# A two-block transformer kernel on one core: tokens turned by VectorE and SBUF copies where TensorE transposed them

## The chip, the cores and the metric

The kernel runs on one core of one Trainium2 chip. The metric is the device time of one execution in microseconds. Three runs of the kernel before took 2508.69 to 2509.17 us, with a median of 2508.91 us.

## The reference

All values are float32. One sequence of T = 256 tokens with D = 2048 features goes through two blocks, one layer each.

First block: `h = rmsnorm(x)`; `proj = h @ w_in` (2048 x 9216) gives u, v (gated mixing over chunks of 128 tokens, 8 groups), q, k, v (8 heads of 128, stick-breaking attention) and two gates; `merged = sigmoid(g_a) * (y_a @ w_up_a) + sigmoid(g_b) * (y_b @ w_up_b)`; `x += merged @ w_o`; then `x += (silu(gate) * up) @ w_ffn_out` with a hidden width of 5632; then `x += sigmoid(rmsnorm(x) @ w_ple_gate) * (p @ w_ple)`.

Second block: `z = rmsnorm(x) @ w_in_2` feeds a causal convolution of width 3, a pooling branch with trailing means, and cross attention (4 heads) on 256 memory rows; `x += mix @ w_out`; then `u = causal_dwconv(h @ w_up) + b`, `x += (silu(gate) * val) @ w_down`; a last rmsnorm.

Nearly all arithmetic is in the products with the weights, 470 MB of which are read once.

## The kernel before, in words

**The stream.** All weight products are cut into 878 granules of 512 KB (128 partitions x 1024 values). A chunk of 8 granules (22 for the two down projections, 4 for w_up_a and w_up_b, 1 for w_ple and the pooling) gives 512 output columns for all 256 tokens, with the tokens on the partitions, in two PSUM banks. For each granule SP loads it into one of RAW = 6 buffers `raw` (`fetch`), ScalarE rounds it to float32r (`wh`, line 1327), VectorE computes the rest `wl = raw - wh` (line 1328), both in a ring of RING = 4, and TensorE does 12 matmuls of 512 columns (`multiply`, lines 1291 and 1297: hi x hi, hi x lo, lo x hi). The last of a granule, line 1297, signals that its ring slot is free.

**The order.** The program is written by one loop over steps. At step s it emits, each on its own engine's queue: the cast and the rest of granule s; the load of granule s + RAW, which waits for the rest of granule s; all work that was put at step s by `at(s, fn)`; and last the 12 matmuls of granule s - 3. Each queue runs in the order of emission. The cast of granule s waits for the last matmul of granule s - 4. A chunk whose last granule is `last` is drained by its `after` at step s = last + 4.

**Turning.** The next product needs its operand with the features on the partitions. `turn` does that: eight TensorE transposes (four in `after_ffn1`, where a chunk gives 256 useful columns) of 128x128 into PSUM banks 4 to 7 (line 374), put at s + 2 or later. ScalarE and VectorE then read those banks and write the operand's `hi` and `lo` parts. The uses: `after_u` (2 chunks), `after_qk` (4), `after_ub` (4, `merged`), `unfold` (16: the residual chunks of w_o, w_ffn_out and w_out, and those of `after_ple`; it writes x1g, x2g, x4g, x3g), `after_ffn1` (22), `after_z` (8) and `after_ffn2` (22). With four transposes in each of the 22 these are 536 transposes, as much as 67 full turns.

**Stages in order of time:** w_in (18 chunks, with attention beside the last ones), w_up_a/w_up_b by turns, w_o, w_ffn_in, w_ffn_out, w_ple_gate/w_ple, w_kv, w_in2 (7 chunks, cross attention `xhead` and pooling beside), w_out with two pooling products, w_up2, w_down. Where the last chunk of a stage feeds the next one, the granules of the next one take its features in order, so that the last features turned (k = 12 to 15) are needed from the next stage's 7th granule on. `late_loads` fetches 2 MB of memory rows at the change to w_ple_gate.

Of the kernel before, what the change touches and what calls it, by code (L numbers as in the profile page):

```python
# [7 lines left out]
P = 128  # L8
T = 256
# [4 lines left out]
RAW = 6  # L14
RING = 4
# [20 lines left out]
MIX_ORDER = (12, 14, 0, 6, 2, 8, 10, 4)  # L36
# [77 lines left out]
def two_block_kernel(nc, t, out):  # L114
# [5 lines left out]
    with ExitStack() as ctx:  # L120
# [26 lines left out]
        o_i = reserve(512)  # L147
        assert NCONST * 4 <= 2560 and place[0] <= nc.sbuf_usable_end
# [12 lines left out]
        ident = view("ident", [P, P], o_i)  # L161
        TA = tmp[:, 0:1024]
# [22 lines left out]
        def parts(name, off_hi, off_lo, n):  # L185
# [44 lines left out]
            "s_attn", "s_cst", "s_mats", "s_misc", "s_late", "s_mem", "s_out", "s_ident", "s_x", "s_gf"))  # L230
        sp = Queue(sem("s_sp"))
# [304 lines left out]
        def after_u(n):  # L536
            def after(s, chunk):
# [9 lines left out]
                def b():  # L547
                    g["t"] = rows_tok[n] = turn(rows, g["u"], 4, 4)
                    u_tok[n] = [act.do(lambda e, i=i: e.copy(
                        U[:, 4 * n + 2 * i:4 * n + 2 * i + 2, :].rearrange("p k t -> p (k t)"), ps[:, 4 + i, :]), g["t"])  # L550
                        for i in range(2)]
                    bank_free[4], bank_free[5] = u_tok[n]
                a()
                at(s + 2, b)
# [54 lines left out]
        def after_qk(dst, g_ap, n):  # L609
            def after(s, chunk):  # L610
# [27 lines left out]
                def f():  # L638
                    rows_tok[n] = g["t"] = turn(rows, g["r"], 4, 4)
                    for i in range(2):  # L640
                        qk_tok.append(act.do(lambda e, i=i: e.activation(
                            dst[:, 4 * n + 2 * i:4 * n + 2 * i + 2, :].rearrange("p k t -> p (k t)"), ps[:, 4 + i, :],
                            ACT.Copy, scale=g_ap), g["t"], got_mats["gq"]))
                    bank_free[4], bank_free[5] = qk_tok[-2:]
# [4 lines left out]
                at(s + 5, f)  # L649
# [125 lines left out]
        def after_ub(n):  # L775
            def after(s, chunk):
                bk = 4 + 2 * (n % 2)
# [5 lines left out]

                def a():
                    done = st_tok["free"] = turn(ST, m, bk, 4)
                    for i in range(2):
                        c = 4 * n + 2 * i
                        hi_ = merged.hi[:, c:c + 2, :].rearrange("p k t -> p (k t)")
                        lo_ = merged.lo[:, c:c + 2, :].rearrange("p k t -> p (k t)")
                        hi = act.do(lambda e, i=i, hi_=hi_: e.copy(hi_, ps[:, bk + i, :]), done)  # L790
                        tk = dve.do(lambda e, i=i, hi_=hi_, lo_=lo_: e.tensor_tensor(
                            lo_, ps[:, bk + i, :], hi_.bitcast(F32), ALU.subtract), hi)
                        merged.ready[c] = merged.ready[c + 1] = bank_free[bk + i] = tk
                at(s + 2, a)
# [10 lines left out]
        def after_ffn1(n):  # L805
            def after(s, chunk):
                bk = 4 + n % 2
                g = {}
                hi = act1.hi[:, 2 * n:2 * n + 2, :].rearrange("p k t -> p (k t)")
                lo = act1.lo[:, 2 * n:2 * n + 2, :].rearrange("p k t -> p (k t)")  # L810
# [638 lines left out]
```

How the kernel before makes its waits and increments, by code:

```python
    def wait(self, tokens):  # L52
        for token in tokens:
            if token is None:
                continue
            if isinstance(token, list):
                self.wait(token)
                continue
            sem, value = token
            if self.waited.get(sem.name, 0) < value:
                self.waited[sem.name] = value
                self.ops.append(lambda e, s=sem, v=value: e.wait_ge(s, v))
# [1 line left out]
    def do(self, fn, *tokens):  # L64
        self.wait(tokens)
        self.n += 1
        self.ops.append(lambda e: fn(e).then_inc(self.sem, 1))
        return (self.sem, self.n)
# [17 lines left out]
    def load(self, sem, dst, src, *tokens):  # L86
        self.count[sem.name] = self.count.get(sem.name, 0) + 16
        self.queue.plain(lambda e: e.dma_start(dst, src).then_inc(sem, 16), *tokens)
        return (sem, self.count[sem.name])
```

## Time and profile before

| what | value |
|---|---|
| median of 3 runs | 2508.91 us |
| profiled execution, its own time | 2509.36 us |
| its span | 2507.2 us |
| TensorE busy | 2486.9 us (99%) |
| VectorE busy | 1403.4 us (56%) |
| ScalarE busy | 1244.4 us (50%) |
| SP's DMA queue, share of 16 engines | 62.2% |
| granted TensorE clock | 0.999 |

The span is the time from the first to the last instruction of the profiled execution, and its own time is 2.2 us more. Busy times of different engines lie beside each other. A matmul's recorded duration (389 ns) is longer than the distance to the next one, because they are pipelined; the distance between starts tells the pace.

### The profile page before, as it was taken

The numbers are of one execution on the slowest core, as the hardware profiler recorded it, in microseconds if no ns is written. First come the engines' busy times: TensorE is split into PE (matmuls) and PEld (weight loads), VectorE is DVE, ScalarE is ACT, GpSimd is POOL, SyncE is SP. The second block draws the span as 40 slices with busy tenths as digits, with TensorE's granted clock in tenths as the row PEclk, the third lists the DMA queues.
The fourth block names the chain that finished last, engine by engine and source line by source line (L and its number), as shares of the span: only waits on it lengthen the run. The fifth ranks groups of instructions, "written<-read, shape, count | busy, mean of one in ns | idle before, by whom it ended". The sixth has DMA issues, their size and how long they took to land.

```text
span 2507.2 us, 27926 instructions
## 1 busy us (share of the span) xinstructions
PE 2486.9 (99%) x11322; PEld 2065.1 (82%) x11322; DVE 1403.4 (56%) x1668; ACT 1244.4 (50%) x1531; POOL 0.2 (0%) x4
## 2 busy tenths in 40 slices
PE   9999999999999999999999999999999999999998
PEld 7888888888888888888888788888888888888886
DVE  7564555655555455544445654765566665665544
ACT  7554666445444444444445654444555555554443
POOL 0000000000000000000000000000000000000000
PEclk9999999999999999999999999999999999999999
DMA  8656666666666666666666565566666666666663
GB/s 287 185 180 188 193 187 178 192 185 185 187 191 189 189 190 188 192 186 192 192 189 225 171 186 178 168 190 186 180 191 185 184 184 191 185 184 209 194 193 128
DMA packets 131105, 473.55 MB, mean 189 GB/s; under 512 B 14624, under 2 KB 15008, under 8 KB 130720
## 3 DMA queue, kind: packets, MB, share of 16 engines
q1 hardware_dynamic: 130976, 471.77, 62.2%
q8 instruction: 89, 1.46, 0.2%
q14 instruction: 40, 0.33, 0.0%
HBM read 469.61 MB, written 2.10 MB: 188 GB/s over the span
## 4 chain that ended last, share of the span: by engine, by line
PE 98%; ACT 1%; DVE 1%; DMA 0%; issue 0%; SPq 0%; DVEq 0%; ACTq 0%
PE ps L1291 86%; PE ps L1297 8%; PE ps L374 2%; ACT wh L1327 0%; DMA raw<-in_w_in 0%; DVE wl L1328 0%; PE ps L732 0%; PE ps L703 0%; PE ps L748 0%; PE ps L580 0%; PE ps L958 0%; PE ps L994 0%; DVE X L881 0%; DVE tmp L876 0%; PE ps L705 0%
## 5 line engine op out<-in xcount | busy, mean ns | idle before, releaser
L1328 DVE TENSOR_TENSOR wl<-raw,wh 128x1024 fp32r<-128x1024 f32 x877 | 1074.0, 1225 | 1076.9 <-ACT wh L1327 1076.6
L1327 ACT CAST wh<-raw 128x1024 fp32r<-128x1024 f32 x877 | 922.6, 1052 | 1171.4 <-PE ps L1297 1168.1
L1291 PE MATMUL ps<-wh,x1g_hi 128*128 128x512 f32 x704 | 276.1, 392 | 0.0
L1291 PE MATMUL ps<-wh,x4g_hi 128*128 128x512 f32 x704 | 276.0, 392 | 0.0
L1291 PE MATMUL ps<-wh,act_hi 128*128 128x512 f32 x704 | 274.3, 390 | 0.0
L1291 PE MATMUL ps<-wl,x1g_hi 128*128 128x512 f32 x704 | 274.0, 389 | 0.0
L1291 PE MATMUL ps<-wl,x4g_hi 128*128 128x512 f32 x704 | 273.9, 389 | 0.0
L1291 PE MATMUL ps<-wl,act_hi 128*128 128x512 f32 x704 | 273.9, 389 | 0.0
L1291 PE MATMUL ps<-wh,h_hi 128*128 128x512 f32 x576 | 227.0, 394 | 2.3 <-DVE wl L1322 1.3
L1291 PE MATMUL ps<-wl,h_hi 128*128 128x512 f32 x576 | 224.1, 389 | 0.0
L1291 PE MATMUL ps<-wh,x1g_lo 128*128 128x512 f32 x528 | 205.7, 390 | 0.0
L1291 PE MATMUL ps<-wh,x4g_lo 128*128 128x512 f32 x528 | 205.6, 389 | 0.0
L1291 PE MATMUL ps<-wh,act_lo 128*128 128x512 f32 x528 | 205.4, 389 | 0.0
L1291 PE MATMUL ps<-wh,h_lo 128*128 128x512 f32 x432 | 168.4, 390 | 0.0
L1291 PEld LDWEIGHTS ps<-wh,act_hi 128*128 128x128 f32 x704 | 132.1, 188 | 27.3
L1291 PEld LDWEIGHTS ps<-wl,act_hi 128*128 128x128 f32 x704 | 132.2, 188 | 27.2
L1291 PEld LDWEIGHTS ps<-wl,x1g_hi 128*128 128x128 f32 x704 | 132.2, 188 | 26.9
L1291 PEld LDWEIGHTS ps<-wl,x4g_hi 128*128 128x128 f32 x704 | 132.2, 188 | 26.8
L1291 PEld LDWEIGHTS ps<-wh,x1g_hi 128*128 128x128 f32 x704 | 132.2, 188 | 26.8
L1291 PEld LDWEIGHTS ps<-wh,x4g_hi 128*128 128x128 f32 x704 | 132.2, 188 | 26.7
L1291 PEld LDWEIGHTS ps<-wh,h_hi 128*128 128x128 f32 x576 | 108.2, 188 | 24.4 <-DVE wl L1322 1.5
L1291 PEld LDWEIGHTS ps<-wl,h_hi 128*128 128x128 f32 x576 | 108.3, 188 | 21.7
(271 smaller groups left out, 3147.4 us busy)
## 6 DMA issues: line engine op xcount, KB each, us to landing
raw<-in_w_in SPq DMA_DIRECT2D x200, 512.0 KB, 3.6
raw<-in_w_ffn_in SPq DMA_DIRECT2D x176, 512.0 KB, 3.6
raw<-in_w_up SPq DMA_DIRECT2D x176, 512.0 KB, 4.2
raw<-in_w_ffn_out SPq DMA_DIRECT2D x88, 512.0 KB, 3.6
raw<-in_w_down SPq DMA_DIRECT2D x88, 512.0 KB, 3.6
raw<-in_w_o SPq DMA_DIRECT2D x32, 512.0 KB, 3.6
raw<-in_w_ple_gate SPq DMA_DIRECT2D x32, 512.0 KB, 3.6
raw<-in_w_out SPq DMA_DIRECT2D x32, 512.0 KB, 3.6
```

Source lines behind the costliest of these rows:

```text
L374: done = pe.do(lambda e, c=c, b=b, at_=at_: e.transpose(ps[:, bk + c // 2, at_:at_ + P], src[:, b, c * P:(c + 1) * P], ident[:]), tok, ban ...
L1291: return e.matmul(*a, start=s, stop=p, skip_group_check=True)
L1297: pe_tok[i] = pe.do(lambda e: e.matmul(dst, lhs, rhs, start=start, stop=stop, skip_group_check=True))
L1327: hi = act.do(lambda e, r=r, slot=slot: e.copy(wh[:, r, :], raw[:, slot, :]), in_tok[s], free)
L1328: lo_tok[s] = dve.do(lambda e, r=r, slot=slot: e.tensor_tensor(wl[:, r, :], raw[:, slot, :], wh[:, r, :].bitcast(F32), ALU.subtract), hi)
```

## The change

`turn` no longer uses TensorE. Two VectorE transposes of 128x512 (one for each half of the tokens) turn every 32x32 block of the rows inside its own quarter of the partitions and write a buffer Y of 4 KB per partition. Sixteen DMAs on SP's queue, each of 32 partitions x 1 KB in runs of 512 B (32 KB), carry the blocks between the quarters into a buffer Z. They are emitted in four groups of four (`move`): two groups at the step of the turn and two at the next one (`steps` = 2: `after_u`, `after_ub`, `unfold`, `after_z`, 30 turns), or one group at each of four steps (`steps` = 4: `after_qk`, `after_ffn1`, `after_ffn2`, 37 turns). All wait for the second VectorE transpose. ScalarE and VectorE read Z, in SBUF, where they read PSUM. What was at s + 2 is now at s + 1 (the VectorE transposes) and s + 5 (the reading of Z); in `after_ffn1` and `after_ffn2` it is s + 1 and s + 7, in `after_qk` s + 4 and s + 10. `after_ffn1` collects two chunks in ST and turns once for both, and `after_ffn2` first copies Z to Y. Y and Z take the place of two raw buffers: RAW is 4. `xhead`, pooling and convolution start two or three steps later, and w_out takes its operands in another order. The transposes of attention probabilities in `xhead` (line 984) stay on TensorE.

```diff
+RAW = 4
 RING = 4
...
+MIX_ORDER = (12, 14, 0, 6, 8, 10, 2, 4)
 
...
+        o_y = reserve(4096)
+        o_z = reserve(4096)
...
+        Y = view("Y", [P, 1024], o_y)
+        Z = view("Z", [P, 1024], o_z)
+        YF = Y.rearrange("p (c t) -> p c t", c=4)
+        YQ = Y.rearrange("p (q g c j) -> p q g c j", q=4, g=2, c=4)
+        ZT = Z.rearrange("p (g c j) -> p c g j", g=8, c=4)
+        ZA = Z.rearrange("p (g a e) -> p g a e", g=2, a=4)
...
-        def turn(src, tok, bk, n):
-
-            done = None
-            for c in range(n):
-                for b in range(2):
-                    at_ = (c % 2) * T + b * P
-                    done = pe.do(lambda e, c=c, b=b, at_=at_: e.transpose(
-                        ps[:, bk + c // 2, at_:at_ + P], src[:, b, c * P:(c + 1) * P], ident[:]),
-                        tok, bank_free[bk], bank_free[bk + 1] if n > 2 else None, got_mats["ident"])
-            return done
-
-        def turned(bk, c):
-            return ps[:, bk + c // 2, (c % 2) * T:(c % 2 + 1) * T]
+        turned = {"n": 0, "y": [], "z": []}
+
+        def turn(step, src, steps, *tokens):
+
+
+
+
+            sem_ = s_turn[turned["n"] % 4]
+            turned["n"] += 1
+            for b in range(2):
+                done = dve.do(lambda e, b=b: e.transpose(YQ[:, :, b].rearrange("p q c j -> p c q j"),
+                                                         src[:, b, :].rearrange("p (c q j) -> p c q j", c=4, q=4)),
+                              *tokens, turned["y"])
+            turned["rows"] = done
+            moved = turned["y"] = []
+            free = turned["z"]
+
+            def move(a):
+                for q in range(4):
+                    token = loads.load(sem_, ZA[32 * q:32 * q + 32, :, a, :],
+                                       Y[32 * a:32 * a + 32, 256 * q:256 * q + 256].rearrange("p (g e) -> p g e", g=2),
+                                       done, free)
+                if a == 3:
+                    moved.append(token)
+
+            for a in range(4):
+                if a * steps < 4:
+                    move(a)
+                else:
+                    at(step + a * steps // 4, lambda a=a: move(a))
+            return moved
+
+        def tiles(x):
+
+            return x.rearrange("p c (g j) -> p c g j", g=8)
 
         def unfold(s, n, tok, gname, dest, free, norm):
 
-            bk = 6 if norm is norm4 else 4 + 2 * (n % 2)
             g = {}
 
...
             def a():
                 squares(n, tok, norm)
+                g["t"] = turn(s + 1, X[:, :, 512 * n:512 * n + 512], 2, tok)
 
             def b():
-                g["t"] = turn(X[:, :, 512 * n:512 * n + 512], tok, bk, 4)
                 for i in range(4):
                     c = 4 * n + i
-                    hi = act.do(lambda e, c=c, i=i: e.activation(dest.hi[:, c, :], turned(bk, i), ACT.Copy,
-                                                                 scale=gain(gname, c)), g["t"], free())
-                    if i % 2 == 0:
-                        continue
-                    for j in (i - 1, i):
-                        dest.ready[4 * n + j] = dve.do(lambda e, c=4 * n + j, j=j: e.scalar_tensor_tensor(
-                            dest.lo[:, c, :], turned(bk, j), gain(gname, c), dest.hi[:, c, :].bitcast(F32),
-                            ALU.mult, ALU.subtract), hi)
-                bank_free[bk] = bank_free[bk + 1] = [hi, dest.ready[c]]
+                    hi = act.do(lambda e, c=c, i=i: e.activation(tiles(dest.hi[:, c:c + 1, :]), ZT[:, i:i + 1],
+                                                                 ACT.Copy, scale=gain(gname, c)), g["t"], free())
+                    dest.ready[c] = dve.do(lambda e, c=c, i=i: e.scalar_tensor_tensor(
+                        tiles(dest.lo[:, c:c + 1, :]), ZT[:, i:i + 1], gain(gname, c),
+                        tiles(dest.hi[:, c:c + 1, :]).bitcast(F32), ALU.mult, ALU.subtract), hi)
+                turned["z"] = [hi, dest.ready[c]]
 
             at(s + 1, a)
-            at(s + 2, b)
+            at(s + 5, b)
             if n == 3:
                 at(s + 3, lambda: rows_root(norm))
                 at(s + 4, lambda: rows_invert(norm))
...
+                    g["t"] = turn(s + 1, ST, 2, m)
+                    st_tok["free"] = turned["rows"]
+
+                def b():
+                    hi = act.do(lambda e: e.copy(tiles(merged.hi[:, 4 * n:4 * n + 4, :]), ZT), g["t"])
+                    lo = dve.do(lambda e: e.tensor_tensor(
+                        tiles(merged.lo[:, 4 * n:4 * n + 4, :]), ZT,
+                        tiles(merged.hi[:, 4 * n:4 * n + 4, :]).bitcast(F32), ALU.subtract), hi)
+                    turned["z"] = lo
+                    for c in range(4 * n, 4 * n + 4):
+                        merged.ready[c] = lo
+                at(s + 1, a)
+                at(s + 5, b)
...
                 def a():
-                    g["t"] = st_tok["free"] = turn(ST, g["m"], bk, 2)
+                    g["t"] = turn(s + 1, ST, 4, g["m"])
+                    st_tok["free"] = turned["rows"]
 
                 def b():
-                    g["hi"] = act.do(lambda e: e.copy(hi, ps[:, bk, :]), g["t"])
+                    c = 2 * n - 2
+                    g["hi"] = act.do(lambda e: e.copy(tiles(act1.hi[:, c:c + 4, :]), ZT), g["t"])
 
                 def c():
-                    tk = dve.do(lambda e: e.tensor_tensor(lo, ps[:, bk, :], hi.bitcast(F32), ALU.subtract), g["hi"])
-                    bank_free[bk] = tk
-                    act1.ready[2 * n] = act1.ready[2 * n + 1] = tk
-                d = 2 if n == 0 else 0
-                at(s + d, z)
-                at(s + d + 2, a)
-                at(s + d + 2, b)
-                at(s + d + 3, c)
+                    c = 2 * n - 2
+                    tk = dve.do(lambda e: e.tensor_tensor(tiles(act1.lo[:, c:c + 4, :]), ZT,
+                                                          tiles(act1.hi[:, c:c + 4, :]).bitcast(F32), ALU.subtract),
+                                g["hi"])
+                    turned["z"] = tk
+                    for k in range(c, c + 4):
+                        act1.ready[k] = tk
+                z()
+                if n % 2:
+                    at(s + 1, a)
+                    at(s + 7, b)
+                    at(s + 8, c)
...
-                    done = rows2_tok["free"] = turn(rows2, g["st"], 6, 4)
+                    g["t"] = turn(s + 1, rows2, 2, g["st"])
+                    rows2_tok["free"] = turned["rows"]
...
-        x_at = first_z[0].last + RING + 4
-        pool_at = first_z[2].last + RING + 4
+        x_at = first_z[0].last + RING + 6
+        pool_at = first_z[2].last + RING + 6
...
                 def y():
-                    g["t"] = st_tok["free"] = turn(ST, g["st"], bk, 4)
+                    g["t"] = turn(s + 1, ST, 4, g["st"])
+                    st_tok["free"] = turned["rows"]
                 hi = act2.hi[:, 2 * n:2 * n + 2, :].rearrange("p k t -> p (k t)")
                 lo = act2.lo[:, 2 * n:2 * n + 2, :].rearrange("p k t -> p (k t)")
 
                 def a():
-                    g["c"] = [act.do(lambda e, c=c: e.activation(C[:, c, :], F[:, c, :], ACT.Identity,
+                    g["f"] = act.do(lambda e: e.copy(tiles(YF), ZT), g["t"])
+                    g["c"] = [act.do(lambda e, c=c: e.activation(C[:, c, :], YF[:, c, :], ACT.Identity,
                                                                  scale=gain("fconv", 176 + 4 * n + c),
-                                                                 bias=gain("fbias", 4 * n + c)), g["t"], part_tok["tb"])
+                                                                 bias=gain("fbias", 4 * n + c)), g["f"], part_tok["tb"])
                               for c in range(4)]
...
-                w = 3 if n == 0 else 0
-                at(s + w, z)
-                at(s + w + 2, y)
+                z()
+                at(s + 1, y)
                 for i, fn in enumerate((a, b, c_, d, f, h)):
-                    at(s + w + 2 + i, fn)
+                    at(s + 7 + i, fn)
...
         for i in range(RAW):
             load_x(i)
             fetch(i)
+        for i in range(RAW, 6):
+            load_x(i)
```

## Rows read from the trace of the kernel before

**Rows 1.** The page: busy time of an engine; shares of the last chain by line.
```profile
PE 2486.9 (99%) x11322; PEld 2065.1 (82%) x11322; DVE 1403.4 (56%) x1668; ACT 1244.4 (50%) x1531; POOL 0.2 (0%) x4
...
PE ps L1291 86%; PE ps L1297 8%; PE ps L374 2%; ACT wh L1327 0%; DMA raw<-in_w_in 0%; DVE wl L1328 0%; PE ps L732 0%; PE ps L703 0%; PE ps L748 0%; PE ps L580 0%; PE ps L958 0%; PE ps L994 0%; DVE X L881 0%; DVE tmp L876 0%; PE ps L705 0%
```

**Rows 2.** Timeline of PE in w_up2: start us, duration us, line, tiles, count.
```profile
2009.36 0.39 PE L1297 MATMUL ps<-wh,x4g_lo 128*128 128x512 f32 x1
...
2012.08 0.40 PE L1297 MATMUL ps<-wh,x4g_lo 128*128 128x512 f32 x1
2012.31 1.04 PE L374 MATMUL ps<-ident,tmp 128*128 128x128 f32 x8
...
2015.72 0.39 PE L1297 MATMUL ps<-wh,x4g_lo 128*128 128x512 f32 x1
```

**Rows 3.** Line 374 alone (ns min/median/max), and who PE waited for (us, times, longest).
```profile
L374 PE MATMUL ps<-ident,tmp x296: 270/272/273, 456.0 to 2262.5; 128*128 128x128 f32 x148
...
PE ps L374 <- DVE X L881: 3.8, 2, 3.4
```

**Rows 4.** Stretches: us, then busy us of PE, PEld, DVE, ACT, POOL; clock, DMA share, GB/s.
```profile
1341.00:1449.00 108.00, 102.83 (x470) 84.75 (x469) 71.91 (x103) 67.48 (x101) 0.00 (x0) 1.00 0.62 198
...
1757.00:2258.00 501.00, 501.00 (x2299) 416.50 (x2299) 308.85 (x400) 276.64 (x357) 0.00 (x0) 1.00 0.62 186
```

**Rows 5.** The page's costliest groups: busy us, mean ns of one, idle before it and releaser.
```profile
L1328 DVE TENSOR_TENSOR wl<-raw,wh 128x1024 fp32r<-128x1024 f32 x877 | 1074.0, 1225 | 1076.9 <-ACT wh L1327 1076.6
L1327 ACT CAST wh<-raw 128x1024 fp32r<-128x1024 f32 x877 | 922.6, 1052 | 1171.4 <-PE ps L1297 1168.1
```

**Rows 6.** Timelines of ACT and of DVE where w_o gives way to w_ffn_in.
```profile
609.53 1.05 ACT L1327 CAST wh<-raw 128x1024 fp32r<-128x1024 f32 x1 [1.67 <-PE ps L1297]
612.25 1.06 ACT L1327 CAST wh<-raw 128x1024 fp32r<-128x1024 f32 x1 [1.67 <-PE ps L1297]
...
613.34 1.23 DVE L1328 TENSOR_TENSOR wl<-raw,wh 128x1024 fp32r<-128x1024 f32 x1 [0.30 <-ACT wh L1327]
```

**Rows 7.** Groups of instructions on DVE and on ACT, shapes kept apart.
```profile
L989 DVE COPY tmp<-ps 128x512 f32<-128x512 f32 x4 | 2.7, 684 | 0.0
...
L399 DVE SCALAR_TENSOR_TENSOR x1g_lo<-ps,cst,x1g_hi 128x256 fp32r<-128x256 f32 x16 | 6.6, 476 | 0.0
...
L338 ACT ACTIVATE mg_hi<-MR,cst 128x256 fp32r<-128x256 f32 x16 | 6.8, 498 | 0.0
```

**Rows 8.** Timeline of SP's queue at the start: start us, duration us of an issue.
```profile
2.11 0.43 SPq L88 DMA_DIRECT2D XT<-in_xt  x1
2.59 0.43 SPq L88 DMA_DIRECT2D raw<-in_w_in  x1
...
4.89 0.68 SPq L88 DMA_DIRECT2D raw<-in_w_in  x1
...
11.16 0.33 SPq L88 DMA_DIRECT2D raw<-in_w_in  x1
```

**Rows 9.** The DMA view: queue's share; issues with count, KB each, median us to landing.
```profile
q1 hardware_dynamic: 130976, 471.77, 62.2%
...
raw<-in_w_in SPq DMA_DIRECT2D x200, 512.0 KB, 3.6
...
MR<-in_mem SPq DMA_DIRECT2D x1, 2048.0 KB, 9.9
...
ident<-in_ident SPq DMA_DIRECT2D x1, 64.0 KB, 4.8
cst<-in_cst SPq DMA_DIRECT2D x1, 8.0 KB, 1.9
```

**Rows 10.** Timeline of DVE at the starts of w_o and of w_out.
```profile
523.61 1.22 DVE L1328 TENSOR_TENSOR wl<-raw,wh 128x1024 fp32r<-128x1024 f32 x1
...
1666.75 0.48 DVE L1105 TENSOR_SCALAR mix_hi<-ps,cst 128x256 fp32r<-128x256 f32 x1
...
1669.49 1.22 DVE L1328 TENSOR_TENSOR wl<-raw,wh 128x1024 fp32r<-128x1024 f32 x1
```

More of the change, by code:

```diff
@@ L13 @@
 EPS = 1e-6
-RAW = 6
+RAW = 4
 RING = 4
@@ L230, in two_block_kernel @@
             "s_attn", "s_cst", "s_mats", "s_misc", "s_late", "s_mem", "s_out", "s_ident", "s_x", "s_gf"))
+        s_turn = [sem(f"s_turn{i}") for i in range(4)]
         sp = Queue(sem("s_sp"))
@@ L547, in b, with c @@
                 def b():
[L548 to L552, printed above, removed]
-                a()
-                at(s + 2, b)
+                    g["t"] = turn(s + 1, rows, 2, g["u"])
+                    rows_tok[n] = turned["rows"]
+                def c():
+                    u_tok[n] = turned["z"] = act.do(lambda e: e.copy(tiles(U[:, 4 * n:4 * n + 4, :]), ZT), g["t"])
+                a()
+                at(s + 1, b)
+                at(s + 5, c)
             return after
@@ L638, in f, with h @@
                 def f():
[L639 to L644, printed above, removed]
+                    g["t"] = turn(s + 4, rows, 4, g["r"])
+                    rows_tok[n] = turned["rows"]
+                def h():
+                    turned["z"] = act.do(lambda e: e.activation(tiles(dst[:, 4 * n:4 * n + 4, :]), ZT, ACT.Copy,
+                                                                scale=g_ap), g["t"], got_mats["gq"])
+                    qk_tok.append(turned["z"])
                 a()
@@ L648, in after @@
                 at(s + 3, d)
-                at(s + 5, f)
+                at(s + 4, f)
+                at(s + 10, h)
             return after
@@ L782, in after @@
                 m = dve.do(lambda e: e.tensor_tensor(ST, ST, SG[:, n, :, :], ALU.add), tok, ua_tok[n])
+                g = {}
                 def a():
[L785 to L794, printed above, removed]
+                    g["t"] = turn(s + 1, ST, 2, m)
[10 more added lines that the diff above has]
+                at(s + 5, b)
             return after
@@ L816, in z @@
                     g["m"] = [dve.do(lambda e, b=b: e.scalar_tensor_tensor(
-                        ST[:, b, 0:T], banks(chunk)[b][:, T:2 * T], RT[:, b:b + 1], ST[:, b, 0:T], ALU.mult, ALU.mult),
-                        g["s"][b], chunk.done) for b in range(2)]
+                        ST[:, b, h0:h0 + T], banks(chunk)[b][:, T:2 * T], RT[:, b:b + 1], ST[:, b, h0:h0 + T], ALU.mult,
+                        ALU.mult), g["s"][b], chunk.done) for b in range(2)]
                     chunk.drained = g["s"] + g["m"]
                 def a():
-                    g["t"] = st_tok["free"] = turn(ST, g["m"], bk, 2)
+                    g["t"] = turn(s + 1, ST, 4, g["m"])
+                    st_tok["free"] = turned["rows"]
                 def b():
-                    g["hi"] = act.do(lambda e: e.copy(hi, ps[:, bk, :]), g["t"])
+                    c = 2 * n - 2
+                    g["hi"] = act.do(lambda e: e.copy(tiles(act1.hi[:, c:c + 4, :]), ZT), g["t"])
                 def c():
-                    tk = dve.do(lambda e: e.tensor_tensor(lo, ps[:, bk, :], hi.bitcast(F32), ALU.subtract), g["hi"])
-                    bank_free[bk] = tk
-                    act1.ready[2 * n] = act1.ready[2 * n + 1] = tk
-                d = 2 if n == 0 else 0
-                at(s + d, z)
-                at(s + d + 2, a)
-                at(s + d + 2, b)
-                at(s + d + 3, c)
+                    c = 2 * n - 2
[10 more added lines that the diff above has]
+                    at(s + 8, c)
             return after
@@ L869, in z @@
                         st_tok["free"]) for b in range(2)]
-                at(s + (2 if n == 0 else 0), z)
+                z()
             return after
@@ L1093, in two_block_kernel @@
                 if what == "u":
-                    conv_taps(ch.last + RING + 3 + i, j)
+                    conv_taps(ch.last + RING + 6 + i, j)
                 else:
-                    conv_split(ch.last + RING + 3, j)
-        conv_taps(first_z[2].last + RING + 3, 0)
+                    conv_split(ch.last + RING + 6, j)
+        conv_taps(first_z[2].last + RING + 6, 0)
         def after_pool(q):
@@ L1148, in b @@
                         o = dve.do(lambda e, c=c: e.scalar_tensor_tensor(
-                            C[:, c, 1:], F[:, c, 0:T - 1], gain("fconv", 88 + 4 * n + c), C[:, c, 1:],
+                            C[:, c, 1:], YF[:, c, 0:T - 1], gain("fconv", 88 + 4 * n + c), C[:, c, 1:],
                             ALU.mult, ALU.add), g["c"][c])
@@ L1153, in b @@
                         g["o"][c] = dve.do(lambda e, c=c: e.scalar_tensor_tensor(
-                            C[:, c, 2:], F[:, c, 0:T - 2], gain("fconv", 4 * n + c), C[:, c, 2:],
+                            C[:, c, 2:], YF[:, c, 0:T - 2], gain("fconv", 4 * n + c), C[:, c, 2:],
                             ALU.mult, ALU.add), g["o"][c])
-                    bank_free[bk] = bank_free[bk + 1] = [g["c"], g["o"]]
+                    turned["y"] = [g["c"], g["o"]]
                 def c_():
```

33 lines of the change are left out of this document (15 added, 18 removed).

## The prediction

> **What bounds the kernel now.** First the page. TensorE is busy for 99% of the span and the chain that ended last runs through its matmuls; 2% of that chain is line 374, the transposes. VectorE and ScalarE are near one half [rows 1]. Next the pace in steady state: the last matmuls of two granules start at 2009.36 and 2012.08, so a granule takes 2.72 us, and the 878 of them 2388 us. With a turn between them the same distance is 15.72 - 12.08 = 3.64 us, so eight transposes cost the bound engine 0.92 us [rows 2]. The feeders' largest idle time is waiting for TensorE: ScalarE's casts for 1168 us on line 1297, VectorE's rests for 1077 us on those casts [rows 5]. So TensorE sets the time, and a microsecond taken from it is a microsecond of the span, until something else comes late.
>
> **What goes.** The 536 transposes that the code issues (296 of them from `tmp`, 0.27 us each with its drain, one pipelined behind the other [rows 3]) are 67 turns of eight: 67 x 0.92 = 61.6 us. The turns of the w_ple stage also made TensorE wait 3.8 us for an addition on VectorE [rows 3], in a stage where it stands idle 108.00 - 102.83 = 5.2 us [rows 4]. In the changed kernel that addition is waited for by VectorE itself. Gain: 65.4 us.
>
> **What comes on VectorE and ScalarE.** 134 block transposes of 128x512. No row shows one. A copy of that shape takes 0.684 us; an operation on half the columns 0.476 [rows 7], on twice the columns 1.225 [rows 5]. I take the copy, 1.37 us a turn, 92 us in all, and keep 0.95 to 2.45 us as its ends. In w_up2 VectorE is busy 308.85 of 501 us [rows 4]; 1.37 us in each chunk of 21.8 raises 62% to 68%. There ScalarE gets a copy of 1024 columns per chunk, about a cast's 1.05 us [rows 5], on 55%. Both hide behind TensorE: the rest of a granule is ready early. Call 0 the moment TensorE ends granule s - 3. The cast of granule s + 1 starts then (612.25) and its rest ends at 613.34 + 1.23, which is 2.35 [rows 6]; TensorE wants it three granules later, at 8.2. That leaves 5.8 us. If this cover were gone each microsecond more would show; the worst burst, eight operations of 0.48 us in `after_ffn2` followed by the next turn, is 3.8 + 1.4 and is spread over two steps, so it stays inside. The other edits to these engines (one cast of 1024 for two of 512, SBUF for PSUM as a source: 0.498 us for 256 columns from SBUF [rows 7]) are worth some tenths beside TensorE: nothing, whichever way.
>
> **What comes on SP's queue.** 16 issues a turn. They start 0.48 us apart when nothing is waited for (2.11, 2.59), and last 0.33 to 0.68 us [rows 8]; I take 0.47, 7.5 us a turn. They wait for the second block transpose, and SP's next `fetch` stands behind them. In a two-step turn: the transposes end at 2.35 + 1.37 = 3.7; eight issues, a fetch, eight issues; the last one starts at about 11.3. The fetch of granule s + 7 leaves at 11.8 where its rest of s + 3 was ready at 7.8: 4 us late. It lands 3.6 us later [rows 9], at 15.4, and the cast wants it at 6 x 2.72 = 16.3. So four raw buffers hold, with 0.9 us before ScalarE waits and 5.8 more before TensorE does; six buffers would have had 5.4 more. Four-step turns put four issues and a fetch (2.3 us) in a step of 2.72 and keep up. At the start of the kernel the fifth load must now wait for the first rest; until the fifth cast lie three more casts of 1.05 us [rows 5] and six operations of about 0.50 [rows 7] on ScalarE, 6.2 us, against 3.6 to land: nothing.
>
> DMA engines: a turn moves 512 KB, as much as one granule, so 67 more loads on 878. With 62.2% [rows 9] for those, even double time for short packets adds under 10 points: covered.
>
> **What is late next.** In the middle of a stage nobody needs Z soon. At the joints somebody does, since reading Z has moved from step s + 2 to s + 5, by three granules, and what is read must have landed. No row shows a 32 KB move between partitions. 8 KB landed 1.9 us after its issue, 64 KB behind other loads 4.8 [rows 9]. I take 2.5, near the first. Then Z is complete at 11.3 + 2.5 = 13.8; the last features are due when TensorE begins the stage's seventh granule, at 5 x 2.72 = 13.6.
> - w_o to w_ffn_in, w_out to w_up2: two casts of 0.50 and a rest of 0.48 [rows 7] for k = 12, 13: 15.3, late by 1.7 each.
> - w_ffn_out to w_ple_gate: the same, and the 2 MB of memory rows (9.9 us to landing [rows 9]) are issued just before the moves. Up to 4 us of queue; most is worked off by the last move. 2.5.
> - w_up_b to w_o: VectorE's rest of s + 1 ends later, at 524.83 [rows 10], 1.05 after the other joints; then one cast of 1024 and one rest of 1024, 1.05 + 1.23: 17.1, late by 3.5.
> - first chunk of w_in2 to `xhead`: its first product is put at s + 6, ahead of the same granule at 13.6, and needs two copies of 512 columns, 1.1 together: 14.9, late by 1.3.
> - last chunk of w_in2 to w_out: pooling work holds VectorE for 2.75 us (1666.75 to 1669.49 [rows 10]) ahead of the block transposes. The moves end at 14.1, the fetch of s + 7 behind them lands at about 18.5, cast and rest of it end at 20.8, the convolution's rest of 0.68 at 21.5; TensorE wants that at 7 x 2.72 = 19.0. Late by 2.5.
>
> Sum of the waits: 1.7 + 1.7 + 2.5 + 3.5 + 1.3 + 2.5 = 13.2 us. With 0.33 us an issue, 1.9 to landing and the shortest transposes it is about 1; each microsecond by which the last move lands later costs 6.
>
> **The sum.** 2509.36 - 65.4 + 13.2 = 2457.2 for an execution like the profiled one; the median of the runs is 0.45 lower, so 2457.
>
> **A rule weighed.** The turns are now made where a copy of 512 columns takes 0.684 us, against 0.92 us for 1024 columns on TensorE. The Trainium skill ("VectorE: DVE Perf Modes", sections "The three transpose paths" and "Rules for kernel authors") gives 390 ns for a 128x128 transpose on TensorE and 311 ns for 32x32 blocks of that size on VectorE, and advises TensorE for 128x128 where PSUM will do. By its 311 ns a turn would be an estimated 2.5 us on VectorE, each joint 1.1 us later, the time 2464. It speaks against the change as if both engines were equally short of time; the rows say they are not.
>
> **Rivals.**
> - *Block transposes at half the copy's pace.* 1.37 us each, 1.37 later at six joints: +8, so 2465. For: it is a reordering, not a copy, and its writes go in pieces of 32. Against: every 512-column row of VectorE in this trace is near 0.68. 0.12.
> - *The moves land late.* Issues at 0.68 us when the queue is loaded (that is what they took at 4.89 [rows 8]) or 4.8 us to landing: 2 to 4 us more at six joints, 2470 to 2481. For: sixteen small ones on one queue, with loads of 512 KB between. Against: in steady state SP's issues lie 2.7 us apart and find the queue empty. 0.10.
> - *No joint is late.* 2509 - 65 + 1 = 2445. Needs both low ends. 0.04.
> - *SP's queue becomes the bound: slower than before.* In a two-step turn the fetch of s + 7 leaves at 4.2 + 16 X for an issue of X us, and 3.6 + 1.05 + 1.23 later its rest is ready; TensorE wants it at 9 x 2.72 = 24.5. So from X = 0.9 on TensorE stops in every such turn, by 16 us per us of X, and the gain is eaten at 65.4 / 30 = 2.2 us a turn, X = 1.03. At X = 1.05: 30 x 2.4 = 72, the four-step turns 12 more: 2509 - 65 + 13 + 84 = 2541. For: 1072 issues are new, and only four buffers are left to cover them. Against: no issue in the trace lasted over 0.68. 0.03.
> - *The change doesn't bring what it removes.* If casts and rests, not matmuls, set the 2.72 us, the transposes lay in a gap: 2505 to 2513. Against: the distance grew by 0.92 us with them. 0.03.
>
> **Chances and range.** The forecast keeps 0.68. A measurement of this kernel can tell about 0.2% (5 us) from no change. Faster by more than that: 0.68 + 0.12 + 0.10 + 0.04 = 0.94; within it 0.03; slower 0.03. The range goes from 2446, almost no wait, to 2474, half of the late case; that leaves out the slow half of that case, the last two rivals and a little of the low end.
>
> **What would show it.** Right: no line-374 rows; granules 2.72 us apart without exception in w_up2; six short waits of TensorE at the joints, together 5 to 25 us, put down to VectorE's rests of `merged`, `x1g`, `x2g`, `x4g`, `mix` and to ScalarE's copy into Z1; block transposes near 0.68 us; ScalarE waiting for the moves about 2 us in two-step turns. Wrong: waits of TensorE for `wl` in the middle of stages, ScalarE waiting for `raw` by more than 5 us, issues on SP over 0.9 us, or a granule's pace other than 2.72 us (by more traffic in SBUF, say).

## The result and the profile after

The changed kernel takes 2586.89 us (median of 4 runs, 2586.43 to 2590.0) against 2508.9 us before: ratio 1.031, 95% interval 1.030 to 1.033. It is 78 us slower where 52 us faster was forecast. The profiled execution took 2587.17 us, with a span of 2585.4 us and a mean granted clock of 0.985 (0.999 before).

The page's busy times and the shares of the last chain, which answer to [rows 1]:

```profile
PE 2468.1 (95%) x10786; PEld 2026.6 (78%) x10786; DVE 1473.0 (57%) x1787; ACT 1259.3 (49%) x1526; POOL 0.2 (0%) x4
...
PE 67%; DVE 10%; SPq 7%; DMA 7%; ACT 6%; issue 3%; DVEq 0%; ACTq 0%
PE ps L1332 61%; SPq L88 7%; PE ps L1338 5%; DVE wl L1371 5%; ACT wh L1370 3%; DMA Z<-Y 3%; DMA raw<-in_w_up 2%; ACT tmp L1181 1%; DVE tmp L1190 1%; DVE Y L387 1%; DVE tmp L1195 1%; ACT Y L1180 1%; DMA raw<-in_w_ple_gate 0%; DVE tmp L1204 0%; DMA raw<-in_w_out 0%
```

The transposes are gone (10786 matmuls where 11322 were), and the chain now leaves TensorE for a third of the span: it goes through SP's queue, the moves, the copies and the rests. TensorE stands idle 2585.4 - 2468.1 = 117.3 us; before it was 20.3. Whom TensorE waited for (us in total, times, longest), the answer to the last of [rows 3]:

```profile
PE ps L1332 <- DVE wl L1371: 64.4, 42, 3.3
PE ps L1332 <- DVE merged_lo L821: 8.4, 1, 8.4
PE ps L1332 <- DVE x4g_lo L426: 5.4, 1, 5.4
PE ps L1332 <- DVE x1g_lo L426: 5.3, 1, 5.3
PE ps L1332 <- DVE x2g_lo L426: 5.2, 1, 5.2
PE ps L1332 <- DVE mix_lo L1125: 3.7, 1, 3.7
PE ps L1332 <- DVE mix_lo L1149: 3.6, 1, 3.6
PE ps L999 <- ACT Z L959: 3.4, 1, 3.4
```

The last seven are at the joints, where one stage gives way to the next: 35.0 us. The first is in the middle of stages, and 48.0 of its 64.4 us lie in w_up2. One stage and a piece of it, as in [rows 4] (us; busy us of PE, PEld, DVE, ACT, POOL; clock; DMA share; GB/s):

```profile
1775.00:2330.00 555.00, 501.63 (x2123) 402.84 (x2122) 328.58 (x438) 292.52 (x374) 0.00 (x0) 0.98 0.61 188
...
1901.00:1926.00 25.00, 22.09 (x85) 17.63 (x84) 13.80 (x20) 12.93 (x17) 0.00 (x0) 0.86 0.59 173
...
1912.00:1916.00 4.00, 4.00 (x11) 3.04 (x11) 4.00 (x7) 2.52 (x3) 0.00 (x0) 0.50 0.39 122
```

w_up2 takes 555 us where it took 501, and there are stretches in which TensorE was granted the lower of its two levels, 1.2 GHz (0.50 in the last row). A mean of 0.985 over 2585 us is 39 us of work lost to half clock. Where TensorE neither waits nor is slowed, a granule takes 2.72 us as before. The distance between the first two of these rows shows it, and the third is one of the waits:

```profile
2005.73 0.39 PE L1338 MATMUL ps<-wh,x4g_lo 128*128 128x512 f32 x1
...
2008.45 0.39 PE L1338 MATMUL ps<-wh,x4g_lo 128*128 128x512 f32 x1
2010.52 0.50 PE L1332 MATMUL ps<-wh,x4g_hi 128*128 128x512 f32 x1 [1.68 <-DVE wl L1371]
```

What the new operations cost: first the block transposes (busy, mean ns), then SP's issues of moves and of loads (ns min/median/max), the answers to [rows 7] and [rows 8], and the DMA view's row of the moves:

```profile
L387 DVE STREAM_TRANSPOSE Y<-tmp 128x512 f32<-128x512 f32 x74 | 48.0, 686 | 0.0
```

```profile
L88 SPq DMA_DIRECT2D Z<-Y x1072: 585/596/2017, 82.8 to 2355.5; - x179
...
L88 SPq DMA_DIRECT2D raw<-in_w_up x176: 327/432/1669, 1760.2 to 2313.4; - x176
```

```profile
Z<-Y SPq DMA_DIRECT2D x1072, 32.0 KB, 2.4
```

The transposes cost 0.686 us (forecast 0.684), a move lands 2.4 us after its issue (forecast 2.5), and an issue holds SP for 0.60 us and the 0.04 after it (forecast 0.47).

### The profile page after: what moved, and what is told of

It reads as the page before. It is cut to its first block, busy times and chain, and to the rows that moved or that the text cites. A ratio compares the mean times of both kernels' runs of the same rounds, so it can differ in the third digit from the quotient of the medians.

```text
span 2585.4 us, 28127 instructions
## 1 busy us (share of the span) xinstructions
PE 2468.1 (95%) x10786; PEld 2026.6 (78%) x10786; DVE 1473.0 (57%) x1787; ACT 1259.3 (49%) x1526; POOL 0.2 (0%) x4
## 4 chain that ended last, share of the span: by engine, by line
PE 67%; DVE 10%; SPq 7%; DMA 7%; ACT 6%; issue 3%; DVEq 0%; ACTq 0%
PE ps L1332 61%; SPq L88 7%; PE ps L1338 5%; DVE wl L1371 5%; ACT wh L1370 3%; DMA Z<-Y 3%; DMA raw<-in_w_up 2%; ACT tmp L1181 1%; DVE tmp L1190 1%; DVE Y L387 1%; DVE tmp L1195 1%; ACT Y L1180 1%; DMA raw<-in_w_ple_gate 0%; DVE tmp L1204 0%; DMA raw<-in_w_out 0%
## 5 line engine op out<-in xcount | busy, mean ns | idle before, releaser
L1370 ACT CAST wh<-raw 128x1024 fp32r<-128x1024 f32 x877 | 912.2, 1047 | 952.8 <-PE ps L1338 799.8
L1332 PE MATMUL ps<-wh,x4g_hi 128*128 128x512 f32 x704 | 282.4, 401 | 53.4 <-DVE wl L1371 48.0
L1332 PEld LDWEIGHTS ps<-wl,h_hi 128*128 128x128 f32 x576 | 108.2, 188 | 21.8
```

Of the source, the lines that this page charges most:

```text
L1332: return e.matmul(*a, start=s, stop=p, skip_group_check=True)
L1370: hi = act.do(lambda e, r=r, slot=slot: e.copy(wh[:, r, :], raw[:, slot, :]), in_tok[s], free)
```

## The experiments

All times are medians, beside runs of the kernel before on the same chip. The last column tells how long w_up2 takes. Its 176 granules at 2.72 us are 478.7 us, so 478.9 means that nothing is lost there.

| kernel | us | against before | first to last start of `wh,x4g_hi` (w_up2), us |
|---|---|---|---|
| before | 2508.9 | | 498.1 |
| changed | 2586.9 | +78.0 | 552.2 |
| before_raw4 | 2509.0 | +0.1 | 498.1 |
| four_moves | 2453.2 | -55.7 | 478.9 |
| joints_pe | 2542.4 | +33.6 | 540.8 |
| up2_pe | 2532.7 | +23.9 | 504.9 |
| joints_up2_pe | 2491.7 | -17.3 | 498.5 |
| split_queues | 2465.2 | -43.8 | 483.2 |
| pool_joints | 2537.4 | +28.5 | 543.8 |
| turn_first | 2528.6 | +19.7 | 500.9 |
| diagonal_pool | 2498.0 | -10.9 | 510.8 |
| split_joints | 2456.5 | -52.5 | 485.6 |
| split_two_joints | 2461.0 | -47.9 | 483.4 |
| split_joints_first | 2448.6 | -60.3 | 478.9 |

**Four raw buffers alone (before_raw4).**

```diff
-RAW = 6
+RAW = 4
...
         for i in range(RAW):
             load_x(i)
             fetch(i)
+        for i in range(RAW, 6):
+            load_x(i)
```

> The kernel before with four raw buffers in place of six, nothing else. Theory A (the sixteen issues of a turn on SP, 0.63 us each, are what makes loads and moves late): four buffers alone cost nothing, 2507 to 2512 us. Theory B (the ring of four raw buffers is too short by itself): TensorE waits for wl in the middle of stages here too, 2520 us or more.

2509.0 us, ratio 1.000 (0.999 to 1.001). The ring of four costs nothing where SP only loads. Theory B falls.

**A quarter of the issues, the same bytes (four_moves).**

```diff
             def move(a):
-                for q in range(4):
-                    token = loads.load(sem_, ZA[32 * q:32 * q + 32, :, a, :],
-                                       Y[32 * a:32 * a + 32, 256 * q:256 * q + 256].rearrange("p (g e) -> p g e", g=2),
-                                       done, free)
+                token = loads.load(sem_, ZA[:, :, a, :],
+                                   Y[:, 256 * a:256 * a + 256].rearrange("p (g e) -> p g e", g=2), done, free)
```

> The changed kernel, with the sixteen moves of a turn replaced by four DMAs over all 128 partitions: the same bytes, the same runs of 512 B, a quarter of the issues. It leaves out that the blocks cross between the partition quarters. Theory A (issues): 12 x 0.63 = 7.6 us less of SP's queue in each turn, the waits for wl in w_up2 (48 us) vanish, the waits at the joints fall from 35 us to under 5, no half clock is left: 2445 to 2460 us. Theory B' (bytes and short packets on the DMA engines, or the time to landing): 2560 to 2590 us, waits as they are.

2453.2 us, ratio 0.978 (0.976 to 0.980), mean clock 0.997. Its issues on SP and its largest waits of TensorE:

```profile
L88 SPq DMA_DIRECT2D Z<-Y x268: 594/600/1649, 82.8 to 2215.7; - x134
...
L88 SPq DMA_DIRECT2D raw<-in_w_up x176: 327/328/433, 1705.4 to 2183.5; - x176
```

```profile
PE ps L1330 <- DVE x2g_lo L424: 4.7, 1, 4.7
...
PE ps L1330 <- DVE merged_lo L819: 1.0, 1, 1.0
```

A move of four times the bytes holds SP as long as a small one, 0.60 us. With 12 issues fewer a turn, no wait for `wl` of over 0.4 us is left, and the time is that of the forecast. The bytes, the runs of 512 B, the block transposes and the later reading of Z are all still there. So the cause is the number of issues, not the bytes. (The edit leaves out that blocks cross between the quarters, so it shows a time and is no version to use.) One joint stays, w_ffn_out to w_ple_gate with 4.7 us. There the last move was issued 3.8 us after the 2 MB of memory rows and took 9.7 us to land, where the median is 3.9; that the rows hold it up is read from this order and was not tested.

**The joints by TensorE (joints_pe), w_up2 by TensorE (up2_pe).** In the first `unfold` and `after_ub` for n = 3 and `after_z` for the first and last chunk of w_in2 are the code of before; in the second `after_ffn2` is:

```diff
...
+            if n == 3 and norm is not norm4:
+                at(s + 1, a_pe)
+                at(s + 2, b_pe)
+            else:
+                at(s + 1, a)
+                at(s + 5, b)
...
```

> The changed kernel with the six turns at the joints (last chunk of w_up_b, w_o, w_ffn_out and w_out, first and last chunk of w_in2) done by TensorE as before. Theory A with the clock as an effect of waits: the 35 us of waits at the joints go, 6 x 0.92 = 5.5 us of transposes come, and the stretches of half clock that begin behind these waits go too, some 15 to 20 us: 2535 to 2545 us. If the half clock has another cause than the waits: 2555 to 2560 us. w_up2 stays at about 550 us.

> The changed kernel with the 22 turns of w_up2 done by TensorE as before, all else as changed. Theory A (in w_up2 a loop of moves, copy, rests and loads takes longer than a chunk's 21.8 us): w_up2 goes from 552 to about 505 us (22 x 0.92 = 20 us of transposes, the joint's wait and its half clock stay): 2535 to 2545 us. If w_up2 is slow by the ring of four buffers and not by the turns: its waits for wl stay, 2570 us or more.

2542.4 us (ratio 1.013, 1.011 to 1.015), as expected: 44.5 us less. By their pages TensorE stands idle 85.0 us where it was 117.3. It is busy 2455.6 us where it was 2468.1, although it does 5.5 us of transposes more: those 18 us are clock, whose mean went from 0.985 to 0.994. Apart from the six turns only waits were taken away, so the half clock was mostly an effect of the waits. That the transposes on TensorE aren't what lifts the clock is seen in four_moves, which has none of these and 0.997. up2_pe gave 2532.7 us (1.009, 1.007 to 1.011), 54 us less and 2 us under what was expected. Both together, joints_up2_pe:

> The six joints and the 22 turns of w_up2 on TensorE, the other 39 turns by VectorE and moves on SP. The two edits gained 44.5 and 54.2 us apart; they touch different stretches, so together 2587 - 44.5 - 54.2 = 2488 us, 21 us under the kernel before. If the waits of the one only moved to the other: 2500 us or more.

2491.7 us (0.993, 0.992 to 0.995): the two gains add up within 4 us. This hybrid beats the kernel before without any new queue.

**Half of the moves from GpSimd (split_queues), all of them (pool_joints, with the joints on TensorE).**

```diff
...
+                    on, sm = (pool_loads, semg) if q % 2 else (loads, sem_)
-                    token = loads.load(sem_, ZA[32 * q:32 * q + 32, :, a, :],
+                    token = on.load(sm, ZA[32 * q:32 * q + 32, :, a, :],
...
```

> The changed kernel with half of a turn's sixteen moves issued by GpSimd's queue, which is otherwise empty; same bytes, same sixteen DMAs, same order and waits. Theory A (time that SP's queue is held by issues): SP then has 8 x 0.63 = 5.1 us less per turn, a step of two moves and a fetch takes 1.9 us, and the waits for wl in w_up2 go. If GpSimd issues a move in 1 us or less: 2450 to 2470 us. If it takes 1.5 us or more, the last move is late by that queue instead: 2480 to 2540 us. Rival (sixteen DMAs are dear in themselves, wherever they are issued, by their completions or packets): 2570 us or more.

2465.2 us (0.982, 0.981 to 0.984). The same sixteen DMAs, shared by two queues, give 122 of the 130 us back by which the forecast had missed. It isn't the DMAs; it is the line in which they stand. A move took longer to land than in the changed kernel (3.7 us on either queue, median, where it was 2.4), and the time fell all the same.

> All sixteen moves on GpSimd's queue, the six joints on TensorE. SP then only fetches. Theory A in its narrow form (SP's loads behind the moves do the harm): 2450 to 2460 us even with slow issues, since only Z is late, and within a stage nobody needs it soon. If late moves hold ScalarE's queue (its copy of Z stands before the next casts), it grows with GpSimd's issue time: at 1 us each the moves end 3.7 + 16 + 2.5 = 22 us after the turn where Z is read at 12 to 17.4, and the time is 2500 to 2600 us.

2537.4 us (1.011, 1.010 to 1.013), the second case, though not by its arithmetic: that asked for 1 us an issue, and GpSimd took 0.53. SP's loads were never behind a move here, and it is just 5 us better than joints_pe. So a late Z is enough for the harm. One turn of w_up2 in its chain of waits (start us, us, what), and the issues:

```profile
1989.89 1.30 DVE Y L390 x2
...
1993.45 7.87 POOL Z L88 x15
2001.33 5.34 DMA Z<-Y
...
2006.69 1.06 ACT Y L1259
```

```profile
L88 POOL DMA_DIRECT2D Z<-Y x16: 533/536/541, 1993.5 to 2001.3; - x16
```

GpSimd issues faster than SP (0.53 us), but in this turn it began 2.3 us after the transposes and its last move took 5.3 us to land beside SP's loads. From the start of the transposes to a complete Z it is 16.8 us. This is one of the four late starts among the 22 turns of w_up2; in the other 18 GpSimd began 0.3 us after the transposes. Even so the copy of Z began about 14 us after their end (median), as in joints_pe: what the quicker issues gave, the slower landing took.

**The loop.** Since both ways of being late ended in the same place, the chain of the changed kernel was followed through one chunk of w_up2:

```profile
2003.04 2.04 DMA Z<-Y
...
2005.10 1.06 ACT Y L1180
...
2006.69 1.58 ACT tmp L1181 x3
2008.27 0.95 ACT wh L1370
...
2009.24 1.22 DVE wl L1371
2010.46 1.58 DVE tmp L1190 x4
2012.04 1.24 DVE tmp L1195 x4
...
2014.67 1.30 DVE Y L387 x2
...
2018.55 4.16 DMA raw<-in_w_up
...
2022.73 1.06 ACT wh L1370
...
2023.81 1.24 DVE wl L1371
2025.05 0.43 SPq L88
...
2025.82 0.58 SPq L88
...
2027.72 2.24 DMA Z<-Y
```

And SP's queue beside it (start us, us, count):

```profile
2016.00 2.51 SPq L88 DMA_DIRECT2D Z<-Y  x4
2018.55 0.58 SPq L88 DMA_DIRECT2D raw<-in_w_up  x1
2019.18 2.50 SPq L88 DMA_DIRECT2D Z<-Y  x4
```

Z is complete at 2005.08; then come the copy to Y, the activations, a cast, its rest, the eight taps, another rest, and only at 2014.67 the block transposes of the next chunk, since they stand behind the taps on VectorE and write the Y that the taps read. Then four groups of moves with a load between, 3.17 us a group; the last group also waits for a rest whose raw load left late at 2018.55. The next Z is complete at about 2030. From Z to Z that is 25 us, and over the whole of w_up2 the block transposes follow each other every 25.2 us (median). TensorE needs 21.8. A wait of ScalarE in front of the copy (22 times, 65.8 us, the DMA's) therefore isn't absorbed: each chunk starts where the last one ended.

Two stages of the same kernel side by side show that it is the loop and not the pace of the groups alone. These are the shares of the chain of work that ended last, first in w_up2 (1850 to 2320 us; its smallest shares are not printed), then in w_ffn_in (640 to 1090 us):

```profile
by line: DVE wl L1371 17.9%; SPq L88 13.6%; DMA raw<-in_w_up 12.1%; DMA Z<-Y 10.2%; issue 8.0%; ACT wh L1370 7.4%; ACT tmp L1181 6.5%; DVE tmp L1190 6.4%; DVE tmp L1195 5.0%; DVE Y L387 4.4%; ACT Y L1180 4.3%; DVE tmp L1204 2.0%; PE ps L133
...
by line: PE ps L1332 91.7%; PE ps L1338 8.3%
```

In w_up2 TensorE's matmuls are about 2% of the chain: it closes without them. In w_ffn_in the turns are four-step turns too, with the same 3.2 us a group (they start at 667.35, 670.54, 673.71 and 676.88), and TensorE never waits for `wl` there. A turn comes only every 16 granules, 43.5 us, and no chunk needs the Z of the turn before for its own transposes.

**The loop cut, with all issues left on SP (turn_first).**

```diff
+        YA = view("YA", [P, 4, T], o_b + 84 * K)
...
-                    g["f"] = act.do(lambda e: e.copy(tiles(YF), ZT), g["t"])
+                    g["f"] = act.do(lambda e: e.copy(tiles(YG), ZT), g["t"], ya_tok.get("free"))
...
-                    g["t"] = turn(s + 1, ST, 4, g["st"])
+                    g["t"] = turn(s + (n > 20), ST, 4, g["st"])
...
-                at(s + 1, y)
+                if n > 20:
+                    at(s + 1, y)
+                else:
+                    y()
```

> The changed kernel with one edit in w_up2 alone: the copy of Z goes to 4 KB of their own (the end of act2's lo part, unused until the last chunks) and not back into Y, and the block transposes of a chunk are put at step s, ahead of the eight taps of the chunk before, not behind them. All sixteen moves stay on SP with their 0.63 us, the ring stays at four. Theory C (a closed loop: transposes, 16 issues, landing, copy, activations, rest, taps, and only then the next transposes, longer than the 21.8 us of a chunk): the loop is cut, a late Z no longer makes the next one later, and w_up2 falls from 555 to 485 to 500 us, the whole to 2520 to 2535. Theory A in its open form (SP's issues hold back the loads through the ring of four, loop or no loop): w_up2 stays over 530 us, the whole over 2560.

2528.6 us (1.008, 1.006 to 1.009); w_up2's first to last start falls from 552.2 to 500.9 us. TensorE's waits for `wl` in the whole kernel, against 64.4 before the edit:

```profile
PE ps L1342 <- DVE wl L1381: 24.4, 25, 3.3
```

58 us come back without one issue less. The copy of Z waits for moves in 2 of the 22 turns where it waited in all, and the block transposes are 22.5 us apart (median), not 25.2. Theory C is shown for w_up2; the open form of theory A, which expected over 2560, falls. The edit also puts the transposes a step, 2.72 us, earlier, and no run tells how much of the gain is this lead.

Of the 24.4 us that stay, 15.2 lie outside w_up2, where nothing was changed (16.4 before the edit), and 9.2 in it. There 22.5 us is still more than 21.8, and the chain (1850 to 2260 us) still hardly touches TensorE:

```profile
by line: DMA raw<-in_w_up 16.4%; DVE wl L1381 14.3%; SPq L88 13.8%; issue 9.0%; ACT wh L1380 8.1%; DVE tmp L1194 6.8%; DVE tmp L1199 6.6%; DVE Y L388 5.7%; ACT tmp L1185 5.2%; PE ps L1342 4.9%; ACT YA L1184 4.1%; DMA Z<-Y 2.2%; DVE tmp L121
```

It runs through loads now, which SP issues behind the moves: ScalarE waited 86.1 us for `raw`. So late loads do harm as well; by this chain the 0.7 us a chunk that are left of 3.4 are theirs.

**Twelve issues (diagonal_pool).**

```diff
...
+                    if a == q:
+                        moved.append(gp.do(lambda e, dst=dst, src=src: e.tensor_copy(dst, src), done, free))
+                        continue
...
```

> The changed kernel with the four blocks of a turn that stay in their own quarter copied by GpSimd's own instructions (32 partitions x 256), and twelve moves on SP in place of sixteen. Theory C: the loop gets 4 x 0.63 = 2.5 us shorter, from 25.2 to 22.7 us, against 21.8 that TensorE needs: w_up2 at 500 to 510 us; the joints' waits fall from 35 us by 6 x 2.5 to about 20, with less half clock: 2500 to 2520 us in all. If the price lay in the bytes and not in the issues: 2565 us or more, a quarter of the bytes being gone from the queue.

2498.0 us (0.996, 0.994 to 0.998), w_up2 510.8 us from first to last start. Four issues less give 89 us, 41 of them in w_up2 and the rest at the joints and by the clock (0.996); that is 2 us under the expected range. Between 16, 12 and 4 issues on SP the kernel takes 2587, 2498 and 2453 us. That isn't a straight line. The block transposes of w_up2 follow each other every 25.2, 23.4 and 21.8 us (medians; 22.7 was expected for the second), and at TensorE's own 21.8 nothing is left to gain there: in four_moves the chain through w_up2 is TensorE's matmuls alone.

**Putting it together.**

> The same half of the moves on GpSimd's queue, and the six turns at the joints on TensorE. It has 6 x 0.92 = 5.5 us of transposes more and no waits at the joints. Theory A: 2450 to 2460 us, if half of the moves on each queue land in time within a stage. Against split_queues: 5 us slower if the joints are in time there already, up to 30 us faster if they are not.

> Half of the moves on GpSimd's queue as in split_queues, and TensorE turns only the two joints that still waited there (w_up_b to w_o 2.1 us, w_ffn_out to w_ple_gate 6.3 us), not six. From split_queues (2465.2 us): 8.4 us of waits and up to 4 us of half clock go, 2 x 0.92 = 1.8 us of transposes come: 2453 to 2456 us, level with or up to 3 us under split_joints (2456.5), which pays for four more turns on TensorE and saves 2.0 us of waits with them.

> split_joints (half of the moves on GpSimd, the six joints on TensorE) and turn_first (the loop of w_up2 cut) together. In split_joints ScalarE still waited 26 us for the moves in front of the copy and TensorE 6.7 us for wl. If that wait is what is left: both go, 2449 to 2453 us. If the loop was already shorter than a chunk there and the 6.7 us have another cause: 2455 to 2458 us.

split_joints gave 2456.5 us (0.979, 0.978 to 0.980). split_two_joints missed: 2461.0 (0.980, 0.979 to 0.982), with runs from 2456.5 to 2461.8. Its trace is of the 2456.5 us run, in which x4g's joint waited 2.6 us where it was 0.6 in split_queues; why the other three took 4 to 5 us more is open. Doing fewer joints on TensorE gained nothing. split_joints_first gave 2448.6 us (0.976, 0.974 to 0.977). A wait of ScalarE for moves is no longer among the eight longest waits of the kernel, and TensorE's longest is one of the start:

```profile
PE ps L1421 <- DVE wl L1454: 1.6, 1, 1.6
```

It is 138 us faster than the changed kernel and 60 us faster than the kernel before, and it still makes 61 of the 67 turns with all sixteen moves.

## Why the prediction was wrong

**What bounds the kernel, and the gain: right.** The gain of 65.4 us is there to be had: four_moves, which keeps 7.6 us of waits at the joints, lands 4 us under the forecast, and split_joints_first, which pays 5.5 us for its six joints, 8 us under it.

**VectorE and ScalarE: sized right, used wrongly.** 0.686 us a block transpose, 57% and 49% busy. What was wrong is the sentence that the worst burst "stays inside" 5.8 us. It was checked on the queue of the kernel before, where every chunk starts on time.

**SP's queue: the step that failed.** It has two faults.
- The size. 0.47 us an issue came from the rows of the start, where issues of 0.43 us follow each other; [rows 8] also had 0.68. Measured: 0.64 with its gap, and the load between two groups 0.62, where it was 0.33. "Four-step turns put four issues and a fetch (2.3 us) in a step of 2.72 and keep up" is thus false: they take 3.2. (A load also landed after 4.2 us, not 3.6.) At 0.47 it would have been true, at 0.56 not, and 0.68 stood in my rows; the range of that term crossed the point at which it decides, and I took the middle. By itself this fault cost nothing in w_ffn_in.
- The form. Each step was compared with the time at which it would be due if the chunk before had been on time. The turn of one chunk of w_up2 depends on the taps of the chunk before, by VectorE's order and by Y. That closes a loop of 25 us around a period of 21.8, and a loop has no slack to spend: the excess comes back every chunk. The 5.8 us of cover on VectorE and the 4.9 us that a load has in hand (due at 16.3, landed at 7.8 + 3.6) are there, but they cover a lateness once, not 22 times: w_up2 begins at 1775.8, and TensorE waits for `wl` for the first time at 1861.3, in the fourth chunk, and then in nearly every one. The price: 48.0 us of waits for `wl` in w_up2, forecast 0, and 16.4 more in other stages, which were not followed one by one.

**The joints: right in kind, undersized.** Six were forecast with 13.2 us, seven came with 35.0: `merged` 8.4 for 3.5, x1g 5.3 and x4g 5.4 for 1.7 each, x2g 5.2 for 2.5, the convolution's part of mix 3.7 for 2.5, `xhead` 3.4 for 1.3, and the pooled part of mix 3.6 that I had not seen. (By the prediction's own terms the convolution's part should have been 1.7 and not 2.5: a load that leaves at 14.1 and needs 3.6 us lands at 17.7, not 18.5.) Two terms were too small. From the end of the transposes to a complete Z the sum had 10.1 us; it took 12.1 at `merged` and 12.2 at x1g, by the issues. And the transposes themselves ended 2.6 us later than in the sum at `merged` and 1.4 at x1g. The likely reason is that ScalarE, whose casts VectorE's rests wait for, had waited 7.7 and 5.0 us for the moves of the chunk before, where the prediction had about 2. The two terms together are 4.6 of the 4.9 us that `merged` is over its forecast, and 3.5 of x1g's 3.6; the other joints were not taken apart. The chain at `merged`, from its transposes on:

```profile
521.50 1.23 DVE Y L387 x2
...
522.75 0.59 SPq L88
...
532.32 0.60 SPq L88
...
532.96 1.89 DMA Z<-Y
...
534.87 1.05 ACT merged_hi L820
...
535.95 1.24 DVE merged_lo L821
```

**The clock: not in the sum at all.** I had taken waits at their own length. 39 us of work went to half clock, behind some of the waits of TensorE.

**The sum, mended:** 21.8 us more at the joints, 64.4 in the middle, 39 of clock are 125 of the 130 us between 2457.2 and 2587.2. The page closes the account. TensorE is idle 117.3 us where the forecast had 20.3 - 3.8 + 13.2 = 29.7, and busy 2468.1 us where it had 2486.9 - 61.6 = 2425.3: 87.6 + 42.8 = 130.4.

**The rivals.** "Slower than before" named SP's queue and had 0.03. Its place was right, its point of decision (0.9 us an issue, in the two-step turns) was not: it was worked out for one turn by itself, as the forecast was, and it priced the four-step turns, where the harm was, at a sixth of the two-step ones. "The moves land late" was priced by the same linear rule, 6 us a microsecond, and would have given at most 2481. The rule of the Trainium skill ("VectorE: DVE Perf Modes", section "Rules for kernel authors") took no part. Nor did the 311 ns that its section "The three transpose paths" gives for 128x128 in bf16: at 0.686 us for 512 columns of float32, VectorE needs 0.17 us per 128 columns in this trace.

**Open.** How much of the loss a ring of six would have taken with the new turning could not be tried: Y and Z fill the SBUF that the two buffers gave. And joints_pe shows that the clock follows the waits, not how long or how many of them it takes: 64 us of waits of at most 3.4 us stayed in that kernel, at a mean clock of 0.994.

## What to carry to other kernels

Before a step is called covered, ask whether its lateness comes back to it: follow the chain from the new operation through every queue until it meets itself in the next period, add it up, and compare with the period, not with the slack. Count DMAs by their issues first: sixteen of 32 KB hold a queue four times as long as four of 128 KB do. With the bytes unchanged, a quarter of the issues was worth 134 us here and an idle second queue 122. Where TensorE sets the time, a wait of 5 us on it can cost more than 5 us (taking away 35 us of waits at the joints gained 50 before the transposes were paid), so leave the few turns that the next stage needs at once on the engine that has no queue in front.

## What the runs showed of the hardware that was not expected

- An issue on SP costs by the DMA, not by its bytes: 0.596 us for 32 KB, 0.600 for 128 KB, both in runs of 512 B. A load of 512 KB in rows of 4 KB takes 0.33 us alone (four_moves, median) and 0.58 us right behind a group of moves (SP's queue in w_up2 above).
- GpSimd issued the same moves in 0.533 us each. In w_up2 of pool_joints it began 0.3 us after the transposes in 18 turns and 2.3 us after them in 4; why is open. A move took 3.7 us (median of the kernel) to land there, and 3.7 in split_queues from either queue, against 2.4 from SP in the changed kernel.
- TensorE was at 1.2 GHz for some microseconds behind waits of 1.9 us (until 2212.8), 2.2 us (2086.0), 2.9 us (1909.8) and 8.4 us (537.3) in the changed kernel, but not behind one of 2.6 us (1883.3). The mean clock was 0.985 with 117 us of idle time in 2585, and 0.998 or 0.999 in split_joints and split_joints_first, where TensorE's longest wait was 1.6 us.
